# Attention inputs of a hybrid decoder step: three 128-partition transfers per head in place of six 64-partition ones

## The chip, the core and the metric

The kernel runs on one core of one Trainium2 chip. Its engines are TensorE (PE in the profile; PEld is its weight load), VectorE (DVE), ScalarE (ACT), GpSimd (POOL) and SyncE (SP), beside 16 DMA engines that all queues share. Transfers issued by GpSimd appear in the profile as queue q0 (software_dynamic), those issued by SyncE as q1 (hardware_dynamic). The metric is the device time of one execution in microseconds (us); lower is better.

## The reference, cut to what matters

One layer of inference for 2048 new prompt tokens and 8 sample tokens, model width 1024, all float32. The projection of the normalised input gives q, k and v of 16 heads of 64 values each, a gate, and the inputs of a state-space branch. What matters here is the attention of the prompt: each query reads keys at distances 0, d, ..., window for three pairs (window, dilation) and the three results are merged.

```python
PATTERNS = ((128, 1), (512, 4), (2048, 16))
q = _rmsnorm(q.reshape(heads), q_norm_w)
k = _rmsnorm(k.reshape(heads), k_norm_w)
...
s = jnp.einsum('nqhd,nkhd->nhqk', qi, ki).astype(jnp.float32) * scale + bias
s = jnp.where(valid, s, -jnp.inf)
lse = jax.nn.logsumexp(s, axis=-1)
p = jnp.exp(s - lse[..., None]).astype(vi.dtype)
o = jnp.einsum('nhqk,nkhd->nqhd', p, vi)
...
a = o_attn.reshape(lead + (D_ATTN,)).astype(jnp.float32) * jax.nn.silu(g.astype(jnp.float32))
return x + mixed @ w_out
```

## The kernel before

The program is five stages with a barrier between them: `project`, `attend`, `scan_a`, `decode`, `output`. `project` leaves the normalised q and k in DRAM, split into a high and a low part and transposed, as `scr["qk"]` of shape (4, 1024, 2048): entry 0 is q high, 1 is q low, 2 is k high, 3 is k low; head h owns rows 64h to 64h+63, each row 2048 floats (8192 bytes).

`attend` works head by head, h = 0 to 15. A score needs q high and q low against k high and k low. For that q_st holds q high in partitions 0 to 63 and q low in partitions 64 to 127, while k_hi and k_lo each hold the same 64 rows twice, in both halves; a product over 128 partitions then sums both parts of q (lines 1105 and 1106). All three tiles have two buffers, by h % 2.

Order of the work around the change:

- GpSimd issues the loads. `load_qk(h)` (line 1023) waits until the scores of head h-2 are done, since they read the same buffer, and then issues six transfers of 64 partitions (line 1032). Heads 0, 1 and 2 are loaded at the start of the stage, head h+3 within head h, after `apply_gate(h-1)`. Behind it in GpSimd's order stand a load of v (lines 904 and 906: v_in has three copies, one for each dilation, and one load serves two heads), `invert(h-1)` (line 1043) and `normalise(h-1)` (line 1047).
- TensorE, in `scores(h)`, waits at the first unit of a head for `qk_loaded`. Heads 0 and 1 are scored ahead; the scores of head h+2 are interleaved with `mix(h)`, in which the exponentials are turned and multiplied with v.
- The denominator of a head makes a round trip over DRAM, issued by SyncE in order: den out (963), den_in back (967), then GpSimd inverts, reciprocal out (971), reciprocal back to 64 partitions (975), GpSimd normalises, result stored to `mT` (979). Only then does SyncE come to the row maxima of the next head but one (`tops_out`, 937 to 957), whose return, `ntop_loaded`, releases the exponentials of that head and also the next `load_qk`.
- ScalarE starts head h's accumulator with a copy (1289) that waits until head h-2's result is stored, since acc has two buffers.

Two lines elsewhere are read for comparison: line 1526 in `scan_a`, a load that GpSimd issues to all 128 partitions of the tile ya, with a source written as 4 groups of 32 rows:

```python
return bass.AP(tensor=ap.tensor, offset=(512 * (t // 4) + 4 * (t % 4)) * D + i % 2 * HALF, ap=[[D, 4], [16 * D, 32], [1, HALF]])
```

and the loads of the cached keys in `decode`, which go to 128 partitions with a source of 128 rows.

Of the kernel before, what the change touches and what calls it, by code (L numbers as in the profile page):

```python
# [21 lines left out]
F32 = mybir.dt.float32  # L22
# [6 lines left out]
D = 1024  # L29
SEQ = 2048  # L30
# [5 lines left out]
HD = 64  # L36
# [18 lines left out]
def with_axes(ap, axes, offset=0):  # L55

    return bass.AP(tensor=ap.tensor, offset=ap.offset + offset, ap=[list(ap.ap[0])] + [list(a) for a in axes])
# [735 lines left out]
def attend(nc, io, scr):  # L793
# [45 lines left out]
    with ExitStack() as ctx:  # L839
        def sb(name, shape, dt=F32):  # L840
            return ctx.enter_context(nc.sbuf_tensor(name, shape, dt))

        ident = sb("ident_a", [P, P])
        q_st = sb("q_st", [P, 2, SEQ], F32R)
        k_hi = sb("k_hi", [P, 2, SEQ], F32R)
        k_lo = sb("k_lo", [P, 2, SEQ], F32R)
# [21 lines left out]
        qk_loaded = [sem(f"qk_loaded{b}") for b in range(2)]  # L868
# [29 lines left out]
        def load_v(eng, p, j):  # L898

            src = v_src(p, j)  # L900
            dst = v_in[:, p, HD:HD + TILES * (P + 1)].rearrange("i (t c) -> i t c", c=P + 1)[:, :, 0:P]
            if p == 1:
                for b in range(4):
                    eng.dma_start(dst[:, 4 * b:4 * b + 4, :], src[:, b, :, :]).then_inc(v_loaded[p], 16)
            else:
                eng.dma_start(dst, src).then_inc(v_loaded[p], 16)
# [3 lines left out]
        def o_rows(b):  # L910
            return slice(HD * (1 - b), HD * (2 - b))
# [111 lines left out]
        @block.gpsimd  # L1023
        def _(pool):
            def load_qk(h):

                if h >= 2:
                    pool.wait_ge(front_ready, scores_end[h - 2])
                for half in range(2):
                    rows = slice(half * HD, (half + 1) * HD)  # L1030
                    for dst, x in ((q_st, half), (k_hi, 2), (k_lo, 3)):
                        pool.dma_start(dst[rows, h % 2, :].bitcast(F32), scr["qk"][x, h * HD:(h + 1) * HD, :]).then_inc(qk_loaded[h % 2], 16)

            def apply_gate(h, b, pair):

                pool.wait_ge(o_out[0], 4 * h + 8)
                pool.wait_ge(gate_loaded, 32 * (pair + 1))
                pool.tensor_tensor(acc[o_rows(b), b, :], acc[o_rows(b), b, :], gate[o_rows(b), :], ALU.mult).then_inc(gated, 1)
                pool.wait_ge(gated, h + 1)

            def invert(h):
                pool.wait_ge(den_moved, 64 * h + 32)
                pool.tensor_tensor(den_in[:, :], den_in[:, :], minus_one[:, :], ALU.pow).then_inc(recip_done, 1)

            def normalise(h, b):
                pool.wait_ge(den_moved, 64 * h + 64)
                pool.tensor_tensor(acc[o_rows(b), b, :], acc[o_rows(b), b, :], recip[o_rows(b), :], ALU.mult).then_inc(finished, 1)
                pool.wait_ge(finished, h + 1)

            for h in range(2):  # L1050
                load_qk(h)
            pool.memset(v_in[:, :, 0:HD - 1], 0.0).then_inc(ones_set, 1)
            pool.memset(v_in[:, :, VW - HD:VW], 0.0).then_inc(ones_set, 1)
            pool.memset(with_axes(v_in[:, 0, 0:1], [[VW, 3], [P + 1, TILES + 1]], HD - 1), 1.0).then_inc(ones_set, 1)
            pool.memset(minus_one[:, :], -1.0).then_inc(ones_set, 1)
            pool.wait_ge(ones_set, 4)
            for p in (2, 1, 0):
                load_v(pool, p, 0)
            load_qk(2)
            for h in range(H):  # L1060
                if h >= 1:
                    apply_gate(h - 1, (h - 1) % 2, (h - 1) // 2)
                if h >= 2 and h % 2 == 0:
                    pool.wait_ge(mixed, NG * h)
                    load_v(pool, 0, h // 2)
                if h + 3 < H:
                    pool.wait_ge(ntop_loaded, 32 * (h + 2))
                    load_qk(h + 3)
                if h % 2 == 1 and h + 1 < H:
                    pool.wait_ge(mixed, NG * h + 4)  # L1070
                    load_v(pool, 2, (h + 1) // 2)
                if h >= 1:
                    invert(h - 1)
                if h % 2 == 1 and h + 1 < H:
                    pool.wait_ge(mixed, NG * h + 12)
                    load_v(pool, 1, (h + 1) // 2)
                if h >= 1:
                    normalise(h - 1, (h - 1) % 2)
            apply_gate(H - 1, 1, H // 2 - 1)
            invert(H - 1)  # L1080
            normalise(H - 1, 1)

        @block.tensor
        def _(pe):
            def front_bank(n_before, b):
                pe.wait_ge(front_free, n_before + 1)
                return front[b]

            def scores(h, units=range(UNITS)):
                b = h % 2  # L1090
                if 0 in units:
                    pe.wait_ge(qk_loaded[b], 96 * (h // 2 + 1))
                for u in units:
                    at = place["score", h, u]
                    bank = front_bank(at, at % 2)
                    for s in range(2):
                        p, r, blk, _, prev = tiles[2 * u + s]
                        d = DILATIONS[p]
                        lhs = with_axes(q_st[:, b, 0:1], [[d, P]], P * d * blk + r)
                        if p == 2:  # L1100
                            axes, first = [[1, 2], [16, P]], r - r % 2
                        else:
                            axes, first = [[d, 2 * P]], P * d * max(blk - 1, 0) + r
                        out = bank[:, 2 * P * s:2 * P * (s + 1)]
                        pe.matmul(out, lhs, with_axes(k_hi[:, b, 0:1], axes, first), start=True, stop=False)  # L1105
                        last = pe.matmul(out, lhs, with_axes(k_lo[:, b, 0:1], axes, first), start=False, stop=True)  # L1106
                    last.then_inc(front_ready, 1)
# [15 lines left out]
            def mix(h, b, pair, more=True):  # L1123
# [29 lines left out]
                for g in range(NG + 1):  # L1153
                    if g < NG:
                        turn_lot(g)
                    if g == OUT_AT and h + 1 < H:
                        maxima_out(h + 1)
                    if g == IN_AT and h + 1 < H:
                        maxima_in(h + 1)
                    if more:  # L1160
                        scores(h + 2, units_at.get(g, ()))
                    if g >= 1:
                        multiply(g - 1)

            pe.wait_ge(const_in, 16)
            scores(0)
            maxima_out(0)
            scores(1)
            maxima_in(0)
            for h in range(H):  # L1170
# [1291 lines left out]
```

## Time and profile before

| | us |
|---|---|
| median of 3 runs | 3069.5 (3068.41 to 3078.42) |
| the profiled execution, own time | 3077.13 |
| its span | 3075.5 |
| `attend` in it, from the first load issued to the next stage's first instructions | 1367.5 to 2191.5 |
| TensorE busy over the span | 2683.0 (87%) |

The profile is one execution. Its busy times are sums over a stage; its waits name for each idle stretch of an engine what ended it. The DMA share is the mean busy share of the 16 DMA engines, so 0.50 can be eight engines that work all the time. Of a queue the profile gives megabytes and the time its packets took as a share of 16 engines; the two together give the rate of an engine while it is busy.

### The profile page before, as it was taken

How to read it: one execution, taken by the hardware profiler on the slowest of the kernel's cores; microseconds unless marked ns; L12 is line 12 of the kernel's file. 1: busy time of each engine (PE TensorE's matmuls, PEld its weight loads, DVE VectorE, ACT ScalarE, POOL GpSimd, SP SyncE). 2: the span in 40 equal slices, each digit the busy share in tenths (PEclk: the TensorE clock that was granted, in tenths of full speed). 3: DMA queues.
4: the chain of work that ended last, by engine and by line, in shares of the span. 5: the costliest groups of instructions: out<-in, count | busy, mean ns of one | idle time of the engine just before them, and what ended most of it. 6: DMA issues, size and time to landing. Idle time of an engine off the chain costs nothing. (4 is left out here: it accounts for less than half of the span.)

```text
span 3075.5 us, 43713 instructions
## 1 busy us (share of the span) xinstructions
PE 2683.0 (87%) x16598; PEld 2368.4 (77%) x16598; DVE 1236.7 (40%) x3327; ACT 884.2 (29%) x1935; POOL 875.4 (28%) x679
## 2 busy tenths in 40 slices
PE   7799999999999999977999999999269999405799
PEld 7799999999988888846998889988157777302585
DVE  3245554200000045424656566565245555273321
ACT  3212222222111111112545455456044444100100
POOL 1054555221221222210243433434223333141000
PEclk9999999999999999987999999999689999757899
DMA  4224354421231111126556656563455555383632
GB/s 158 85 70 111 105 147 139 131 71 58 73 121 69 68 55 56 55 76 147 126 122 150 147 132 155 126 145 85 109 173 180 184 168 165 124 323 116 218 148 75
DMA packets 197764, 381.87 MB, mean 124 GB/s; under 512 B 62659, under 2 KB 119979, under 8 KB 184476
## 3 DMA queue, kind: packets, MB, share of 16 engines
q1 hardware_dynamic: 158748, 242.40, 25.3%
q0 software_dynamic: 36160, 132.25, 16.9%
q10 hardware_dynamic: 2672, 4.74, 0.5%
q8 instruction: 119, 1.95, 0.3%
q14 instruction: 65, 0.53, 0.1%
HBM read 259.71 MB, written 124.96 MB: 125 GB/s over the span
## 5 line engine op out<-in xcount | busy, mean ns | idle before, releaser
L118 PE MATMUL bank<-w_hi,hT_hi 128*128 128x256 f32 x1792 | 508.0, 283 | 14.2 <-DMA ident<-ident 11.8
L120 PE MATMUL bank<-w_hi,hT_lo 128*128 128x256 f32 x1792 | 504.7, 282 | 0.0
L119 PE MATMUL bank<-w_lo,hT_hi 128*128 128x256 f32 x1792 | 503.2, 281 | 0.0
L1105 PE MATMUL front<-k_hi,q_st 128*128 128x256 f32 x768 | 316.9, 421 | 42.4 <-DMA k_lo<-qk 29.6
L118 PEld LDWEIGHTS bank<-w_hi,hT_hi 128*128 128x128 f32 x1792 | 338.8, 189 | 15.1 <-DMA ident<-ident 12.1
L1148 PE MATMUL obank<-turned_p,v_in 128*128 128x128 f32 (+1 forms) x1632 | 321.5, 331 | 25.9 <-ACT turned_p L1281 24.8
L120 PEld LDWEIGHTS bank<-w_hi,hT_lo 128*128 128x128 f32 x1792 | 339.2, 189 | 0.0
L119 PEld LDWEIGHTS bank<-w_lo,hT_hi 128*128 128x128 f32 x1792 | 338.7, 189 | 0.0
L1148 PEld LDWEIGHTS obank<-turned_p,v_in 128*128 128x128 f32 x1632 | 271.1, 197 | 44.5 <-ACT turned_p L1281 27.5
L1268 ACT ACTIVATE score<-score,ntop_sb 128x256 f32<-128x256 f32 (+1 forms) x768 | 289.9, 455 | 6.7 <-DMA ntop_t<-ntop 6.5
L1106 PE MATMUL front<-k_lo,q_st 128*128 128x256 f32 x768 | 274.5, 365 | 0.0
L118 PE MATMUL bank<-hT_hi,w_hi 128*128 128x512 f32 (+1 forms) x672 | 265.9, 396 | 0.0
L120 PE MATMUL bank<-hT_hi,w_lo 128*128 128x512 f32 (+1 forms) x672 | 265.7, 395 | 0.0
L119 PE MATMUL bank<-hT_lo,w_hi 128*128 128x512 f32 (+1 forms) x672 | 264.1, 393 | 0.0
L403 POOL TENSOR_TENSOR w_hi<-w_raw,zero 128x256 fp32r<-128x256 f32 (+1 forms) x80 | 100.7, 1259 | 562.1 <-PE bank_s L120 303.9
L1195 DVE CUSTOM_DVE_ANT_0 score<-front,bias_sb 128x256 f32<-128x256 f32 (+1 forms) x768 | 249.3, 363 | 14.0 <-issue 13.1
L1105 PEld LDWEIGHTS front<-k_hi,q_st 128*128 128x128 f32 x768 | 209.9, 273 | 51.4 <-issue 30.0
L1106 PEld LDWEIGHTS front<-k_lo,q_st 128*128 128x128 f32 x768 | 214.3, 279 | 0.0
L1132 PE MATMUL back<-ident_a,score 128*128 128x128 f32 x1200 | 186.0, 276 | 0.0
L420 POOL TENSOR_TENSOR rsq<-msq,mhalf 128x4 f32<-128x4 f32 x128 | 129.5, 1012 | 195.9 <-DVE msq L609 195.7
L1281 ACT COPY turned_p<-back 128x512 f32<-128x512 f32 (+1 forms) x160 | 88.4, 553 | 258.0 <-PE back L1132 257.9
L1132 PEld LDWEIGHTS back<-ident_a,score 128*128 128x128 f32 x1200 | 148.1, 143 | 11.9 <-issue 0.2
(282 smaller groups left out, 4824.5 us busy)
## 6 DMA issues: line engine op xcount, KB each, us to landing
qk<-xc_in SPq DMA_DIRECT2D x64, 512.0 KB, 5.1
w_raw<-w_in POOLq DMA_DIRECT2D x26, 1024.0 KB
q_st<-qk POOLq DMA_DIRECT2D x32, 512.0 KB
k_hi<-qk POOLq DMA_DIRECT2D x32, 512.0 KB
k_lo<-qk POOLq DMA_DIRECT2D x32, 512.0 KB
v_in<-v_out POOLq DMA_DIRECT2D x16, 1024.0 KB, 12.9
cum_all<-cum SPq DMA_DIRECT2D x16, 1024.0 KB, 10.4
xcT<-xc SPq DMA_DIRECT2D x12, 1024.0 KB
```

What stands on the lines that cost most here:

```text
L118: pe.matmul(out, lhs_hi(k), rhs_hi(k), start=k == 0, stop=False)
L119: pe.matmul(out, lhs_hi(k), rhs_lo(k), start=False, stop=False)
L120: last = pe.matmul(out, lhs_lo(k), rhs_hi(k), start=False, stop=k == KT - 1)
L403: pool.tensor_tensor(w_hi[:, b, ks, 0:width], w_raw[:, b, ks, 0:width], with_axes(zero[:, :], [[0, n], [0, width]]), ALU.add).then_inc(w_h ...
L420: pool.tensor_tensor(rsq[:, n % 2, :], msq[:, n % 2, :], mhalf[:, :], ALU.pow).then_inc(q_root, 1)
L1105: pe.matmul(out, lhs, with_axes(k_hi[:, b, 0:1], axes, first), start=True, stop=False)
L1106: last = pe.matmul(out, lhs, with_axes(k_lo[:, b, 0:1], axes, first), start=False, stop=True)
L1132: last = pe.transpose(back[g % 2][:, n * P:(n + 1) * P], score[:, b, at:at + P], ident[:, :])
L1148: last = pe.matmul(obank[m["bank"]][:, m["col"]:m["col"] + m["n"]], v_in[:, p, (P + 1) * m["v"][1] + P * b:(P + 1) * m["v"][1] + P * b + P ...
L1195: last = dve.tensor_tensor_reduce(out=score[:, b, at:at + w], in0=front[place_at % 2][:, 2 * P * s + skip:2 * P * s + skip + w], in1=bias[ ...
L1268: act.activation(score[:, b, at:at + w], score[:, b, at:at + w], ACTF.Exp, bias=ntop[:, b, n:n + 1]).then_inc(exp_done, 1)
L1281: act.copy(turned_p[:, g % 4, 0:n], back[1][:, 0:n]).then_inc(odd_out, 1)
```

## The change

`load_qk` issues three transfers, each to all 128 partitions. The source is written as two groups of 64 rows: for q_st the groups lie 1024 rows apart (q high and q low), for k_hi and k_lo the step between the groups is 0, so the same 64 rows are read twice. The bytes are the same, 3.15 MB a head. `scores` waits for 48 in place of 96 on the semaphore.

```diff
                 if h >= 2:
                     pool.wait_ge(front_ready, scores_end[h - 2])
-                for half in range(2):
-                    rows = slice(half * HD, (half + 1) * HD)
-                    for dst, x in ((q_st, half), (k_hi, 2), (k_lo, 3)):
-                        pool.dma_start(dst[rows, h % 2, :].bitcast(F32), scr["qk"][x, h * HD:(h + 1) * HD, :]).then_inc(qk_loaded[h % 2], 16)
+                for dst, x, apart in ((q_st, 0, D * SEQ), (k_hi, 2, 0), (k_lo, 3, 0)):
+                    first = scr["qk"][x, h * HD:(h + 1) * HD, :]
+                    src = bass.AP(tensor=first.tensor, offset=first.offset, ap=[[apart, 2], [SEQ, HD], [1, SEQ]])
+                    pool.dma_start(dst[:, h % 2, :].bitcast(F32), src).then_inc(qk_loaded[h % 2], 16)
...
                 if 0 in units:
-                    pe.wait_ge(qk_loaded[b], 96 * (h // 2 + 1))
+                    pe.wait_ge(qk_loaded[b], 48 * (h // 2 + 1))
```

The order on TensorE, VectorE, ScalarE and SyncE is unchanged. On GpSimd, inside one head of `attend` (here the loads of a head, then of v, then invert; names are tile<-source and the destination's shape), before:

```order
L1038 TENSOR_TENSOR acc<-acc,gate 64x2048
L1032 DMA q_st<-qk 64x2048
L1032 DMA k_hi<-qk 64x2048
L1032 DMA k_lo<-qk 64x2048
L1032 DMA q_st<-qk 64x2048
L1032 DMA k_hi<-qk 64x2048
L1032 DMA k_lo<-qk 64x2048
L906 DMA v_in<-v_out 128x16x128
L1043 TENSOR_TENSOR den_in<-den_in,minus_one 128x16
```

and after, at the same place on GpSimd:

```order
L1038 TENSOR_TENSOR acc<-acc,gate 64x2048
L1032 DMA q_st<-qk 128x1x2048
L1032 DMA k_hi<-qk 128x1x2048
L1032 DMA k_lo<-qk 128x1x2048
L906 DMA v_in<-v_out 128x16x128
L1043 TENSOR_TENSOR den_in<-den_in,minus_one 128x16
```

Six issues became three and nothing else moved; over the 16 heads GpSimd issues 48 transfers in place of 96. In `scan_a`, further on in GpSimd's list and the same in both kernels, stands the load of ya, which has the same form as the new transfers:

```order
L1521 DMA ma_raw<-mT 128x1024
L1526 DMA ya<-x_all 128x1x512
L1521 DMA ma_raw<-mT 128x1024
L1526 DMA ya<-x_all 128x1x512
```

Nothing moved here; the rows are shown for the shape of ya's transfer.

## Rows read from the trace of the kernel before

**Rows 1.** The page: each engine's busy time and its share of the span.
```profile
PE 2683.0 (87%) x16598; PEld 2368.4 (77%) x16598; DVE 1236.7 (40%) x3327; ACT 884.2 (29%) x1935; POOL 875.4 (28%) x679
```

**Rows 2.** Windows: stretch, length, busy by engine, granted clock, DMA share, GB/s.
```profile
1366.00:1396.00 30.00, 3.78 (x16) 3.62 (x16) 1.57 (x15) 0.00 (x0) 12.10 (x22) 0.50 0.94 206
...
1500.00:1600.00 100.00, 97.35 (x601) 92.72 (x600) 59.65 (x304) 53.71 (x135) 33.42 (x24) 1.00 0.59 136
```

**Rows 3.** TensorE's waits from 1366 to 1500: us in total, times, longest.
```profile
PE front L1105 <- DMA k_lo<-qk: 29.6, 1, 29.6
PE front L1105 <- DVE top L1195: 10.3, 10, 8.3
```

**Rows 4.** Timeline: GpSimd's first load issued, and TensorE's first score.
```profile
1367.49 0.56 POOL L1032 DMA_DIRECT2D q_st<-qk  x1 [70.57 <-POOLq L2353]
...
1392.22 0.56 PE L1105 MATMUL front<-k_hi,q_st 128*128 128x256 f32 x1 [29.64 <-DMA k_lo<-qk]
```

**Rows 5.** Timeline: head 0's maxima sent by SyncE, and back at VectorE.
```profile
1416.10 0.94 SPq L937 DMA_DIRECT2D tops<-top  x2
...
1433.43 0.21 DVE L1214 TENSOR_REDUCE top<-tops_sb 128x16 f32<-128x48 f32 x1 [8.90 <-DMA tops_sb<-tops]
```

**Rows 6.** DMA queues, 1612 to 1620, a load of q and k: packets, MB, share.
```profile
q0 software_dynamic: 260, 1.70, 102.0%
```

**Rows 7.** DMA queues, 2750 to 2790, loads to 128 partitions in `decode`.
```profile
q1 hardware_dynamic: 720, 6.29, 41.2%
```

**Rows 8.** The last two loads of ya: GpSimd's issue, a window, q0 from 2616 to 2624.
```profile
2613.92 1.42 POOL L1526 DMA_DIRECT2D ya<-x_all  x2 [0.30 <-POOL xend L1540]
...
2618.00:2621.00 3.00, 3.00 (x15) 2.49 (x14) 0.00 (x0) 0.00 (x0) 1.74 (x1) 1.00 0.49 135
...
q0 software_dynamic: 544, 0.53, 29.1%
```

**Rows 9.** Timelines of SyncE and GpSimd over two heads.
```profile
1614.26 0.32 SPq L971 DMA_DIRECT2D den<-den_in  x1
1625.85 0.46 SPq L975 DMA_DIRECT2D recip<-den  x1
...
1662.14 0.32 SPq L971 DMA_DIRECT2D den<-den_in  x1
1673.80 0.46 SPq L975 DMA_DIRECT2D recip<-den  x1
...
1606.51 0.60 POOL L1032 DMA_DIRECT2D q_st<-qk  x1 [4.21 <-issue]
...
1635.35 4.55 POOL L1047 TENSOR_TENSOR acc<-acc,recip 64x2048 f32<-64x2048 f32 x1 [14.99 <-DMA recip<-den]
...
1656.06 0.55 POOL L1032 DMA_DIRECT2D q_st<-qk  x1 [10.04 <-DMA ntop_t<-ntop]
...
1678.72 4.56 POOL L1047 TENSOR_TENSOR acc<-acc,recip 64x2048 f32<-64x2048 f32 x1 [16.60 <-DMA recip<-den]
...
1702.20 0.60 POOL L1032 DMA_DIRECT2D q_st<-qk  x1 [4.18 <-issue]
```

**Rows 10.** Timelines, the same steps for head 13, with no load in flight.
```profile
2127.66 0.33 SPq L971 DMA_DIRECT2D den<-den_in  x1
2129.07 0.46 SPq L975 DMA_DIRECT2D recip<-den  x1
...
2133.80 4.53 POOL L1047 TENSOR_TENSOR acc<-acc,recip 64x2048 f32<-64x2048 f32 x1 [6.16 <-DMA recip<-den]
```

**Rows 11.** Waits: TensorE from 1500 to 2190, ScalarE and SyncE from 1500 to 2100.
```profile
PE obank L1148 <- ACT turned_p L1281: 24.8, 9, 4.4
...
ACT acc L1289 <- DMA mT<-acc: 68.9, 12, 9.4
...
SPq L975 <- DMA den<-den_in: 135.3, 13, 11.6
SPq L950 <- DVE ntop_sb L1216: 66.8, 13, 10.4
```

## The prediction, as it was put on record

> **What bounds the kernel now.** I read the page first, then the stage that the change touches, and there the waits. TensorE is busy for 87% of the span [rows 1]; over most of `attend` it is at 97% [rows 2], so a transfer is worth time only where TensorE ends up waiting for it. Three such places exist. (a) At the start of the stage TensorE does nothing until head 0's q and k are there: 29.6 us [rows 3], of which 24.7 us lie between the first load issued at 1367.49 and the first score at 1392.22 [rows 4]; the DMA engines are 94% busy in that stretch (the first of [rows 2]). (b) The first row maxima go out at 1416.10 and are back at 1433.43 [rows 5], 17.3 us for a few kilobytes, and TensorE waits 8.3 of them [rows 3]. (c) After that TensorE never waits for q or k. It waits for a ScalarE copy, 24.8 us in nine places [rows 11], up to 4.4 each, and these stand behind ScalarE's wait for a stored head, 68.9 us in twelve places, up to 9.4. That stored head is the end of the round trip of the denominator, which SyncE issues step by step, so the round trip must be followed.
>
> Rows 9 show it for two heads. With a load of q and k in flight the 8 KB reciprocal takes 11.6 us from its issue to the next issue, in both heads (1614.26 to 1625.85, 1662.14 to 1673.80). With nothing in flight the same step takes 1.4 us [rows 10]. The way back to 64 partitions takes 9.5 us where loads of v are still moving (1625.85 to 1635.35), 4.9 us where the load is over (1673.80 to 1678.72), and 4.7 us in a quiet stretch [rows 10]. Because SyncE works in order, and its list leads on to the row maxima that release the next load, these latencies are in the loop that sets the pace of a pair of heads, 1606.51 to 1702.20 = 95.7 us [rows 9]. The loop has little slack: SyncE waits 66.8/13 = 5.1 us a head for VectorE [rows 11], and not all of that is free.
>
> **What the change does to a load.** The bytes stay. What decides is how many DMA engines carry a transfer and how fast each goes.
>
> Before: from 1612 to 1620 the queue moved 1.70 MB at 102% of 16 engines [rows 6], 1.70/(1.02 x 16 x 8 us) = 13.0 GB/s an engine. To 128 partitions engines do better: 6.29 MB at 41.2% over 40 us [rows 7] is 6.29/(0.412 x 16 x 40) = 23.9 GB/s. So 64 partitions cost about half the rate of an engine, and the change takes that handicap away. A head's 3.15 MB take 3.15/(16 x 0.0130) = 15.1 us now.
>
> After: the nearest row is the load of ya, also issued by GpSimd, also to 128x1xN, with a source in 4 groups. Two of them are in flight from 2618 to 2621, and the DMA share is 0.49 at 135 GB/s [rows 8], eight engines of sixteen: four for each, and two different sets of four. Groups and engines have the same number. The new source has 2 groups, so I take two engines for a transfer, and a different pair for each of the three: six engines for a head. The Trainium skill (DMA: Bandwidth & Descriptors, "Why a DMA increments its semaphore by 16 and not by 1") says that a DMA gets the largest number up to 16 that divides the slowest dimension on both sides, which gives 2 here and 4 for ya. By that rule the row and the forecast agree.
>
> Each of the six engines then carries 3.15/6 = 0.524 MB. At 23.9 GB/s that is 21.9 us. But ya's engines ran slower: 0.53 MB for 29.1% of 16 engines over 8 us [rows 8] is 14.2 GB/s, and at that rate it is 36.9 us; at the 13.0 of rows 6 it would be 40. Why narrow transfers that run side by side are slow the rows do not tell; three that start together and walk through the partitions in the same order may get in each other's way. Bounds 22 and 37 us; I take 29, halfway, because ya's short transfers carry their start-up in that rate. The load of a head gets longer by 14 us although the handicap is gone.
>
> **The sum.** (a) Start: now 24.7 us. After: about 1.5 us until data flow, 29 us for head 0 (head 1 goes to the next six engines at the same time), and a share of SyncE's bias and gate loads, 1.77 MB or 0.11 MB an engine, 4.6 us at 23.9 and 8.5 at 13.0, of which I take 5. Together 35.5: **+11 us**. Bounds 1.5 + 22 + 4.6 = 28, +3.4; 1.5 + 37 + 8.5 = 47, +22.
>
> (b) First maxima: now 17.3 us under a load on all 16 engines. Six busy engines with a quicker pace each should delay less. Between 0 and the 8.3 of the wait I take **-3 us**.
>
> (c) Each of the other loads is issued one head (48 us) before its scores, so even 37 us are hidden. Their cover is that distance; it would be gone at 48. What remains is what a load does to the reciprocal's steps. Such a step needs all the engines, so the slowest counts, and 11.6 - 1.4 = 10.2 us of delay are 16 packets of 8192 bytes at 0.63 us (8192 bytes at 13.0 GB/s). At 29 us for 64 packets a packet takes 0.45, so the delay is 16 x 0.45 = 7.2: the step out takes 8.6, **-3.0** in each head. But the load now lasts into the step back. Where that took 4.9 it takes 4.7 + 7.2 = 11.9, **+7.0**; where it took 9.5, **+2.4**. The maxima after it meet the tail of v's loads, which wait behind q and k on the six engines: I take **+1** a pair. A pair of heads: -6.0 + 7.0 + 2.4 + 1 = +4.4. GpSimd saves three issues of 0.5 us; they stand ahead of a step that waits for other things in one head of two, and I count nothing. From the fourth load to the last there are 12, six pairs, and v's loads extend it a little: 6.5 x 4.4 = **+29 us**.
>
> At 22 us a load: a packet 0.34, delay 5.5; -4.7 twice, +5.3 and +0.7: -3.4 a pair, -22 in all. At 37 us: 0.58, delay 9.3; -0.9 twice, +9.1, +4.5, and up to +4 for the maxima: +16, or +104. So (c) is the large term and its sign turns at a load of about 24 us.
>
> Sum: +11 - 3 + 29 = **+37 us**. On the profiled execution's 3077.1 that is 3114; that execution stands 7.6 us (0.25%) over the median of 3069.5, so on the median **3107 us**.
>
> **Rivals.**
> 1. *The narrow transfers run at full rate* (22 us). For it: rows 7. Against: ya's rate in rows 8. Start +3.4, maxima -3, pairs -22: -22 us, 3048. TensorE can gain no more in a pair than it waits there, some 4 us, so it does not go much lower. This is the case that ends faster; it decides below a load of 24 us.
> 2. *The three transfers crowd each other fully* (37 us). For it: 14.2 GB/s in rows 8. Start +22, pairs +104: about +120, 3190.
> 3. *The transfer is spread over all sixteen engines*, as its 128 destination partitions suggest. Then 3.15 MB take 3.15/(16 x 0.0239) = 8.2 us, the start gets some 10 us shorter (4.9 MB with SyncE's loads in 12.9 + 1.5 against 24.7), the first maxima 5, and the reciprocal is out of the load's way, so that TensorE's 24.8 us go: -40, 3030. Against it: 0.49 for two transfers in rows 8. The Trainium skill (DMA: Bandwidth & Descriptors, "Rules for kernel authors") advises one 128-partition transfer in place of two to disjoint halves. By that rule the time would be this rival's; the same list warns that a slowest dimension under 16 confines a transfer to as many engines.
> 4. *It does not matter*: shorter delay and longer load cancel in (c), with (a) small; a load of 24 to 26 us, 3060 to 3079.
>
> That all three share one pair (66 us a load, no longer hidden behind 48) is ruled out by the two sets of four in rows 8 as far as ya goes; it would cost over 200 us.
>
> **How the numbers follow.** Forecast (load 26 to 34 us) 0.50, rival 2 with all above 34 us 0.20, rival 1 0.14, rival 3 0.06, rival 4 0.10. What a measurement of this kernel can tell from no change is about 0.3%, 9 us. Faster by more: 0.20; within: 0.12 (rival 4 and the edge of the forecast); slower: 0.68. The likeliest case gives 3107, its own range 3080 to 3150. For 8 in 10 the range reaches into rival 1 and to most of rival 2: 3045 to 3180.
>
> **What the profile after would show.** Two engines each: while a load is in flight alone the DMA share is near 6/16 = 0.38 (0.75 when heads 0 and 1 load together), not 1.0; a share of 1.0 at twice the rate would be rival 3. The first score would come 35 us after the first load is issued. SyncE's wait before line 975 would fall from 11.6 to about 9, and GpSimd's before line 1047 rise in the heads where it is short now. The distance between load issues of two heads apart would grow from 95.7 to 100; if it shrinks, (c) has the wrong sign. If TensorE waits for k_lo in later heads too, the loads are longer than a head. I would be wrong most of all if the rate of narrow transfers is not between the two rows, or if the delay of a small transfer is not in proportion to the time of a packet.

## The result, and the profile of the changed kernel

The changed kernel takes 3219.4 us (median of 4 runs, 3213.4 to 3228.1), the kernel before 3071.9 in the same comparison: 1.048 times as long, 95% interval 1.0449 to 1.0511. The direction was forecast, the size was not: +148 us where +37 was expected, and outside the range. The profiled execution has a span of 3226.5 us, 151 more than that of before.

The page first, TensorE's row (it answers to [rows 1]) and the row of GpSimd's queue: packets, MB, share of 16 engines.

```profile
PE 2691.5 (83%) x16598; PEld 2374.5 (74%) x16598; DVE 1231.8 (38%) x3327; ACT 884.6 (27%) x1935; POOL 865.0 (27%) x631
...
q0 software_dynamic: 78400, 132.42, 15.9%
```

TensorE does the same work in 8.5 us more; the rest of the 151 is idle time. (The packets more than doubled, while the megabytes stayed; more on that at the end.) The waits over the stage, from 1366 to 2350, of TensorE, ScalarE and SyncE (us in total, times, longest), beside [rows 3, 11]:

```profile
PE front L1105 <- DMA k_lo<-qk: 179.0, 14, 70.5
PE front L1105 <- DVE top L1195: 21.1, 9, 19.4
PE obank L1148 <- ACT turned_p L1281: 10.2, 9, 2.2
...
ACT acc L1289 <- DMA mT<-acc: 38.9, 7, 6.9
...
SPq L975 <- DMA den<-den_in: 122.0, 16, 13.7
```

The first row carries the result. Before, TensorE waited for k_lo once, 29.6 us; now fourteen times, 179.0 us. One of these is the start (70.5); the other thirteen, one in each later head from the fourth on (head 3, as heads count from 0), sum to 108.5, or 8.3 each. Against [rows 3] the first maxima cost 11.1 us more (19.4 for 8.3), and against [rows 11] the waits for ScalarE's copy are 14.6 us less. So 40.9 + 108.5 + 11.1 - 14.6 + 8.5 = 154 against the 151 us of the span: the loss is located.

The 8.5 us of busy time fit the waits. After head 6's wait of 8.61 us the granted clock is at the lower of its two levels (0.50, 1.2 GHz) for over 4 us, where the kernel before, which does not wait there, has 1.00 (2.4 GHz). The first 4 us with head 6's scores, after and then before (18 matmuls for 21):

```profile
1717.00:1721.00 4.00, 3.91 (x18) 3.74 (x19) 1.53 (x11) 0.92 (x3) 3.48 (x2) 0.50 0.70 178
...
1631.00:1635.00 4.00, 3.80 (x21) 3.52 (x20) 2.61 (x13) 1.39 (x3) 0.00 (x0) 1.00 0.38 69
```

The start, beside [rows 4]: GpSimd's first issue, and TensorE's first score.

```profile
1369.22 0.85 POOL L1032 DMA_DIRECT2D q_st<-qk  x1 [70.56 <-POOLq L2353]
...
1434.79 0.56 PE L1105 MATMUL front<-k_hi,q_st 128*128 128x256 f32 x1 [70.46 <-DMA k_lo<-qk]
```

From issue to score 65.6 us, where it was 24.7. One later load, head 5's:

```profile
1632.83 0.83 POOL L1032 DMA_DIRECT2D q_st<-qk  x1 [18.64 <-DMA ntop_t<-ntop]
...
1662.61 0.59 PE L1105 MATMUL front<-k_hi,q_st 128*128 128x256 f32 x1 [3.85 <-DMA k_lo<-qk]
```

Issue to score is 29.8 us here, and TensorE was late by 3.85. For the next four loads it is 34.4, 31.8, 36.5 and 30.5, always ended by k_lo. Over all thirteen it is 29.8 to 32.7 us in the odd heads and 34.4 to 40.5 in the even ones, where five of v's loads are issued while the load runs; the mean is 34.3. Less TensorE's wait, 25.1 to 26.5 us are left: that is when TensorE would have come to use the data. In the kernel before, head 6 was loaded at 1606.51 and head 7 at 1656.06 [rows 9], and this is TensorE's first score with each:

```profile
1631.04 0.55 PE L1105 MATMUL front<-k_hi,q_st 128*128 128x256 f32 x1
...
1681.97 0.55 PE L1105 MATMUL front<-k_hi,q_st 128*128 128x256 f32 x1
```

No wait is marked, yet the distance from issue to use is 24.5 and 25.9 us, not 48 (23.9 to 26.2 over the thirteen heads). That distance is all the time that a load has before it holds up TensorE; it is called its cover below.

Last, windows (stretch, length, busy by engine, granted clock, DMA share, GB/s): the start, and five microseconds of the later load in which nothing else moves.

```profile
1390.00:1410.00 20.00, 0.00 (x0) 0.00 (x0) 0.00 (x0) 0.00 (x0) 0.00 (x0) 0.50 1.03 124
...
1642.00:1647.00 5.00, 5.00 (x35) 4.78 (x34) 4.18 (x18) 2.60 (x9) 0.00 (x0) 1.00 0.38 158
```

0.38 is six engines of sixteen, as forecast, and 158/6 is 26 GB/s for each. At the start all sixteen are busy, with less moved.

### The profile page after: what moved, and what is told of

Its sections match the earlier page's. It is cut to its first block and busy times, and to the rows that moved or that the text cites. A ratio compares the mean times of both kernels' runs of the same rounds, so it can differ in the third digit from the quotient of the medians.

```text
span 3226.5 us, 43665 instructions
## 1 busy us (share of the span) xinstructions
PE 2691.5 (83%) x16598; PEld 2374.5 (74%) x16598; DVE 1231.8 (38%) x3327; ACT 884.6 (27%) x1935; POOL 865.0 (27%) x631
## 3 DMA queue, kind: packets, MB, share of 16 engines
q0 software_dynamic: 78400, 132.42, 15.9%
## 5 line engine op out<-in xcount | busy, mean ns | idle before, releaser
L1105 PE MATMUL front<-k_hi,q_st 128*128 128x256 f32 x768 | 318.0, 422 | 200.3 <-DMA k_lo<-qk 179.0
L118 PEld LDWEIGHTS bank<-w_hi,hT_hi 128*128 128x128 f32 x1792 | 338.7, 189 | 15.3 <-DMA ident<-ident 11.9
L1148 PEld LDWEIGHTS obank<-turned_p,v_in 128*128 128x128 f32 x1632 | 271.5, 198 | 29.7 <-ACT turned_p L1281 12.9
L1195 DVE CUSTOM_DVE_ANT_0 score<-front,bias_sb 128x256 f32<-128x256 f32 (+1 forms) x768 | 249.3, 363 | 13.9 <-issue 13.0
L1188 DVE MEMSET tick<- 128x1 f32 x384 | 22.7, 59 | 378.4 <-PE front L1106 374.8
```

Source lines behind the costliest of these rows:

```text
L118: pe.matmul(out, lhs_hi(k), rhs_hi(k), start=k == 0, stop=False)
L1148: last = pe.matmul(obank[m["bank"]][:, m["col"]:m["col"] + m["n"]], v_in[:, p, (P + 1) * m["v"][1] + P * b:(P + 1) * m["v"][1] + P * b + P ...
L1195: last = dve.tensor_tensor_reduce(out=score[:, b, at:at + w], in0=front[place_at % 2][:, 2 * P * s + skip:2 * P * s + skip + w], in1=bias[ ...
```

## The experiments

Theory after the result: the source's slowest dimension of 2 gives each transfer two engines (such a transfer is called narrow below); the load of a head then takes 30 to 40 us, longer than the 24 to 26 us from its issue to its use, and at the start two such loads and v's slow each other.

**swap**: the three transfers with the 64 rows as the slowest dimension and the two copies inside. The two copies of a row then lie in adjacent partitions, for q and k alike, so the products are unchanged.

```diff
-                    src = bass.AP(tensor=first.tensor, offset=first.offset, ap=[[apart, 2], [SEQ, HD], [1, SEQ]])
+                    src = bass.AP(tensor=first.tensor, offset=first.offset, ap=[[SEQ, HD], [apart, 2], [1, SEQ]])
```

> The changed kernel with one edit: the source's two outer dimensions change places, so it is 64 groups of 2 rows in place of 2 groups of 64, and partition 2i+half holds row i of that half, in q_st, k_hi and k_lo alike. Bytes, issues, destination and waits are the same. Theory (the number of groups sets the number of DMA engines): the load is carried by 16 engines, DMA share near 1.0 while it is in flight, 3.15 MB in 8 to 10 us; first score about 15 us after the first issue; no later wait for k_lo; time 3020 to 3050. Rival (three transfers to 128 partitions are slow as such): the loads stay at 30 to 36 us and the time near 3219.

Measured 3036.3 us, ratio to before 0.9874 (0.9845 to 0.9904), as the theory had it. Its window in a later load, and its waits from 1366 to 2650:

```profile
1640.00:1645.00 5.00, 5.00 (x28) 4.87 (x28) 3.56 (x15) 2.60 (x10) 1.14 (x1) 1.00 1.02 425
...
PE front L1105 <- DMA k_lo<-qk: 23.8, 1, 23.8
PE front L1105 <- DVE top L1195: 7.6, 23, 3.1
PE obank L1148 <- ACT turned_p L1281: 3.2, 4, 1.5
```

Same tiles, same bytes, same three transfers; only the order of the source's dimensions differs. All sixteen engines work, 425 GB/s instead of 158 (and instead of the 210 that [rows 6] give for 64 partitions). The start, the first maxima and ScalarE's copies all cost TensorE less than before: 5.8 + 5.2 + 21.6 us. So the whole loss of the change comes from the order of the source's dimensions, with which go the number of engines and the partitions that each of them writes; and this kernel is 1.3% faster than the one before.

**early**: the changed kernel, with each later load issued at the start of its head, without waiting for the row maxima. This gives the cover of about a head that the prediction had assumed.

```diff
             for h in range(H):
+                if h + 3 < H:
+                    load_qk(h + 3)
...
-                if h + 3 < H:
-                    pool.wait_ge(ntop_loaded, 32 * (h + 2))
-                    load_qk(h + 3)
```

> The changed kernel with load_qk(h+3) issued at the head's start, ahead of apply_gate and without its wait for ntop_loaded (the wait for the scores of head h+1 stays). Theory (a load of 33 us is covered by only 26 us): with some 45 us of cover the 13 later waits for k_lo, 108 us, go, the start stays slow: about 3120, up to 3150 if the earlier load delays the row maxima. Rival (the waits come from the DMA engines being full, so that a load takes as long as the head however early it is issued): waits and time stay near 3219.

Measured 3286.9 us, 1.0691 (1.0664 to 1.0719). The expectation failed, and the rows say how (1366 to 2650):

```profile
PE obank L1147 <- DVE turned_p L1226: 158.6, 15, 25.6
PE front L1104 <- DMA k_lo<-qk: 68.7, 1, 68.7
...
DVE top L1213 <- DMA tops_sb<-tops: 215.4, 14, 28.5
...
SPq L945 <- DMA tops<-top_t: 187.8, 16, 30.0
SPq L975 <- DMA den<-den_in: 17.1, 16, 1.1
```

The thirteen later waits for k_lo are gone, with 52 to 73 us from issue to use: more distance is what they lacked. But the load now lies over the row maxima's way over DRAM, where each small step waits behind it, and TensorE waits for the exponentials instead, 158.6 us. The denominator's step, clear of the load, is down to 1.1 us.

**before_early** does the same to the kernel before.

> The kernel before, with each later load issued at the start of its head, without waiting for the row maxima. The step from den to its reciprocal should come down from 11.6 us to 1.4, as in the run early. If the collision with the row maxima goes by the load's length (15 us here against 30 to 36 in early, which lost 50 us to the changed kernel), the maxima's way back grows by 8 to 12 us a head, of which SyncE's slack of some 5 us a head takes a part: 3080 to 3150. Rival (only loads that outlast the cover collide): 3050 to 3073.

Measured 3077.4, ratio 1.0007 (0.9991 to 1.0024): no difference, and between the two cases of the expectation (3080 to 3150, 3050 to 3073). SyncE's wait for den falls from 138.5 us to 17.8 (16 times each, from 1366 on), its wait at line 945 rises from 54.3 to 113.5, VectorE's wait for the maxima from 12.1 to 66.2, and TensorE's waits only change their name: 22.4 us for VectorE's copy in place of 24.8 for ScalarE's. A load delays whichever round trip it lies on. Moving a load of 15 us is a draw, moving one of 30 or more a loss.

**swap_early** puts the early issue on swap.

> The source of the three transfers written with the 64 rows outside and the two copies inside (as in the run swap, 3036), and besides each later load issued at the start of its head, without waiting for the row maxima. If the collision seen in the run early (small transfers delayed behind a load) scales with the load's length, a load of some 10 to 15 us at full width now lies beside the row maxima's way back: that step grows from about 7 to 12 to 15 us in each head and the kernel takes 3036 + 0 to 40, that is 3035 to 3075. Rival (the early issue takes the load out of the denominator's way, which is what ScalarE and TensorE still wait for): 3015 to 3030.

Measured 3032.7, ratio 0.9853 (0.982 to 0.9886), which overlaps swap's interval; it lies between the two cases expected. With a load of some 8 us neither place hurts: the den step falls from 77.4 to 18.7 us in 16, the maxima's rises from 27.5 to 80.8, and TensorE waits for neither.

**start_only** and **rest_only** divide the change by heads: the three narrow transfers for heads 0 and 1 alone, or for all heads but these, and six transfers for the others.

```diff
+                if h < 2:
+                    for dst, x, apart in ((q_st, 0, D * SEQ), (k_hi, 2, 0), (k_lo, 3, 0)):
...
+                else:
+                    for half in range(2):
...
```

> Three transfers for heads 0 and 1, the old six for heads 2 to 15. Theory (the start costs 41 us and the first row maxima 11, by the traces): 3072 + 50 = 3122, first score 65 us after the first issue. Rival (the start overlaps with what follows and is given back): under 3100.

Measured 3135.8, 1.0194 (1.0155 to 1.0233): 62 us, where 50 were expected. The profile shows the start at 62.5 us from issue to score (1368.58 to 1431.09), the first wait 67.4 (+37.8), 12 us more of TensorE's busy time, and 12 us more of a wait in `scan_a` that no part of the change touches (acc_a, 42.1 for 30.1; it lies between 23 and 42 in these profiles). The first maxima cost 8.6, as before.

> The old six transfers for heads 0 and 1, three for heads 2 to 15. Theory (13 waits for k_lo of 8.3 us each, 108 us, less some 15 us of ScalarE's stalls that go): 3072 + 95 = 3167. Rival (the later waits follow from the late start): close to 3072.

Measured 3206.5, 1.043 (1.0404 to 1.0456): 133 us, where 95 were expected. Two rows from 1366 to 2650:

```profile
PE front L1111 <- DMA k_lo<-qk: 133.7, 14, 29.6
PE front L1111 <- DVE top L1201: 21.1, 10, 19.2
```

The start is as before (29.6), the thirteen others are 104.1 us, and the first maxima wait 19.2. So that last loss belongs to head 2's narrow load, in flight while they travel, and not to those of heads 0 and 1. The two parts sum to 195 us and the whole is 148, so shares are read from the waits and not from these differences. On the profiled executions the parts are 63 and 120 us, 32 more than the 151 of the whole. Of this excess 20 us are waits in `scan_a` (12 and 7 more than before, and 1 less in the changed kernel) and 20 are TensorE's busy time (12.2 and 16.5 more, against 8.5); 7.5 go the other way, as both parts together wait less for k_lo. Why the wait in `scan_a` differs was not found.

**in_turn** and **offset** ask what makes the start slow. in_turn issues head 1's load when head 0's is complete; offset issues it behind v's first loads, 8.7 us after head 0's.

```diff
-            for h in range(2):
-                load_qk(h)
+            load_qk(0)
+            pool.wait_ge(qk_loaded[0], 48)
+            load_qk(1)
```

> The changed kernel, with the load of head 1 issued only when head 0's is complete; nothing else differs. Theory (narrow transfers that are in flight together slow each other, so that 12 engines for two heads take 60 us where a head alone takes 30 to 36): the first score comes 32 to 38 us after the first load is issued instead of 65.6, TensorE's first wait is about 40 us instead of 70.5, a second wait of 5 to 20 us for k_lo follows at head 1, and the kernel takes 3219 - 30 + 12 = about 3200 (3190 to 3210). Rival (a pair of engines is that slow from the stage's other traffic, v's load and SyncE's, or from the first touch of the rows): the first score still comes over 55 us after the issue, head 1 is later still, and the kernel takes 3240 or more.

in_turn took 3209.0 us, 1.0437 (1.0401 to 1.0472), and its first score came 34.3 us after the first issue (1368.01 to 1402.30). Without head 1's load and v's beside it, a head takes at the start what it takes later. Part of the gain goes to a second wait of 13.9 us at head 1.

> The changed kernel, with the load of head 1 issued behind the first loads of v instead of ahead of them, some 8 us later; nothing waits. Theory (transfers that walk through the same partitions at the same moment slow each other, whatever their number): 8 us or more apart, heads 0 and 1 share twelve engines at nearly full pace, the first score comes 30 to 40 us after the first load is issued instead of 65.6, and while both heads load the rate is over 180 GB/s where it was 124 to 137. The kernel takes 3219 - 20 = about 3200 (3185 to 3210), somewhat below in_turn. Rival (it is the number of narrow transfers in flight that counts): the first score comes 50 us or more after the issue, the rate stays under 150 GB/s, and the kernel takes 3210 to 3225.

offset took 3208.9, 1.0414 (1.039 to 1.0437), which the theory's range still holds, but its first score and rate did not come: the first score 54.8 us after the issue (1368.47 to 1423.24), 120 GB/s from 1400 to 1410. An offset of 8.7 us does not free the two heads from each other; the theory of two loads that meet at the same partitions falls in this form. It also clears v, whose loads in_turn had held back together with head 1's: by the sizes of the packets, v's (4096 bytes) move 3 of these 120 GB/s, and q's and k's (8192 bytes) 116. But twelve narrow engines aren't always slow: in in_turn, when the end of head 1's load meets the start of head 2's, the window reads

```profile
1430.00:1435.00 5.00, 0.00 (x0) 0.00 (x0) 0.00 (x0) 0.00 (x0) 0.00 (x0) 0.50 0.74 263
```

twelve engines (0.74) at 22 GB/s each.

**one_narrow**: the kernel before, only k_lo as one narrow transfer behind the four others.

```diff
-                    for dst, x in ((q_st, half), (k_hi, 2), (k_lo, 3)):
+                    for dst, x in ((q_st, half), (k_hi, 2)):
                         pool.dma_start(dst[rows, h % 2, :].bitcast(F32), scr["qk"][x, h * HD:(h + 1) * HD, :]).then_inc(qk_loaded[h % 2], 16)
+                first = scr["qk"][3, h * HD:(h + 1) * HD, :]
+                src = bass.AP(tensor=first.tensor, offset=first.offset, ap=[[0, 2], [SEQ, HD], [1, SEQ]])
+                pool.dma_start(k_lo[:, h % 2, :].bitcast(F32), src).then_inc(qk_loaded[h % 2], 16)
```

> The kernel before, with only k_lo's two transfers of 64 partitions replaced by the narrow one of 128 (q_st and k_hi stay as four transfers on all engines). Theory (three narrow transfers side by side slow each other): alone, a pair of engines carries its 0.52 MB each in 22 to 25 us plus its sixteenth part of the other four transfers, 0.13 MB each or 5 to 10 us, partly overlapped: the load takes 26 to 30 us, which meets the cover of 26 to 28, so the later waits for k_lo stay under 3 us each, and the kernel takes 3075 to 3110. Rival (a pair of engines is slow by itself, 32 us or more for a transfer whatever runs beside it): the load takes 35 us or more, TensorE waits some 8 to 10 us for k_lo in each of 13 heads, and the kernel takes 3180 to 3220.

Measured 3253.9, 1.0574 (1.0529 to 1.0618), worse than three narrow ones, and outside both expectations. Two windows of one load, issued from 1613.92 on:

```profile
1616.00:1626.00 10.00, 10.00 (x58) 9.72 (x57) 7.60 (x31) 5.04 (x16) 3.79 (x3) 1.00 0.96 196
...
1636.00:1641.00 5.00, 3.23 (x24) 2.83 (x22) 3.31 (x12) 1.97 (x5) 3.13 (x1) 1.00 0.12 52
```

First the four wide transfers go on sixteen engines; then two engines (0.12) carry k_lo alone at 26 GB/s each. The pair is not slow: 1.05 MB at 52 GB/s are 20 us. But they come after the 10 us of the others and not beside them, and TensorE waits 152 us in thirteen heads. The expectation had them partly overlapped; here the narrow transfer waits its turn on its engines.

**six_g2**: the kernel before, its six transfers to 64 partitions with each source as 2 groups of 32 rows.

```diff
-                        pool.dma_start(dst[rows, h % 2, :].bitcast(F32), scr["qk"][x, h * HD:(h + 1) * HD, :]).then_inc(qk_loaded[h % 2], 16)
+                        first = scr["qk"][x, h * HD:(h + 1) * HD, :]
+                        src = bass.AP(tensor=first.tensor, offset=first.offset, ap=[[SEQ, 2], [2 * SEQ, HD // 2], [1, SEQ]])
+                        pool.dma_start(dst[rows, h % 2, :].bitcast(F32), src).then_inc(qk_loaded[h % 2], 16)
```

> The kernel before with its six transfers to 64 partitions, but each source written as 2 groups of 32 rows (even rows, then odd rows, the same for q and k, so the products are the same). Theory (the slowest dimension of the source sets the number of engines and each transfer gets another pair): the six transfers of a head take twelve engines, 0.26 MB each; at 13.0 GB/s 20 us, at 26 GB/s 10 us, so the load takes 12 to 22 us, DMA share about 0.75 while it lasts, later waits for k_lo are absent or small, and the kernel takes 3040 to 3100. Rival A (pairs are shared between the halves, six engines a head): 30 us or more, waits for k_lo of 4 to 14 us in each head, 3180 to 3230. Rival B (the 128 partitions mattered, not the groups: 64 partitions keep all 16 engines): DMA share 1.0 during a load, 3065 to 3080.

Measured 3655.4 us, 1.1872 (1.1841 to 1.1904), worse than every expectation. A stretch of the start (with a second load in flight), and one of head 5's load, issued at 1746.50, which is alone:

```profile
1410.00:1430.00 20.00, 0.02 (x1) 0.05 (x1) 0.00 (x0) 0.00 (x0) 0.00 (x0) 0.50 1.24 65
...
1770.00:1780.00 10.00, 0.00 (x0) 0.00 (x0) 0.84 (x2) 0.00 (x0) 0.00 (x0) 0.66 0.79 68
```

Twelve engines (0.79) move 65 to 68 GB/s together, less than half of what six moved in the changed kernel, and a later load takes 57 to 64 us from issue to score. (Of the 1.24 at the start 0.46 are packets of 4 bytes; the 8192-byte packets of q and k are 0.76.) The groups alone, without any transfer to 128 partitions, are enough to ruin the load. Why the pace collapses was still open, and three runs separate source from destination: theory S puts it down to the rows that are read, theory D to the partitions that are written.

**six_near** keeps six_g2's destinations and lets the source step by one row (row 63 is left out).

```diff
-ap=[[SEQ, 2], [2 * SEQ, HD // 2], [1, SEQ]]
+ap=[[(HD // 2 - 1) * SEQ, 2], [SEQ, HD // 2], [1, SEQ]]
```

> The run six_g2 with the same destinations, but the two groups of a source are rows 0 to 31 and rows 31 to 62 (step 1 row inside a group in place of 2); row 63 is left out, so the products are not the reference's. Theory S (the slow pace comes from the source: rows read at the same time in steps of 16 KB): the rate during a load rises from 75 to over 140 GB/s, the load takes under 25 us, later waits for k_lo are small, and the kernel takes 3050 to 3150. Theory D (it comes from the partitions written at the same time, here i, 32+i, 64+i and 96+i): the rate stays at 70 to 85 GB/s and the kernel takes 3600 to 3700. If the groups are merged into one, the DMA share is 1.0 at 210 GB/s and the run says nothing.

Measured 3667.6 (1.1922, interval 1.1862 to 1.1982), and 60 GB/s in the same stretch of the start: theory D, though its rate is below the 70 to 85 GB/s expected.

**stride2** keeps the changed kernel's destinations and lets the source step by two rows (`[2 * SEQ, HD]`), so it reads rows of other heads too.

> The changed kernel with every second row of twice the range as its source (step 16 KB in place of 8 KB), so the values are not the reference's; destinations, bytes and engines are the same. Theory S: the rate of a later load falls from some 140 to 158 GB/s to 75 to 90, the load takes 40 us or more in place of 30 to 36, the waits for k_lo grow by 8 us or more a head, and the kernel takes 3330 to 3450. Theory D: nothing changes, 3200 to 3235.

Measured 3236.6 (1.0521, interval 1.0463 to 1.0579), first score after 66.3 us, waits for k_lo 195.7 us for 179.0: little of the 110 us and more that theory S asked for. 15.5 of the 16.7 us come from head 14 alone (29.7 for 14.2), which waits longer in far_rows too (21.1); the other twelve heads wait 94.8 us for 94.4.

**far_rows** takes head 1's rows from head 9.

> The changed kernel with head 1's rows taken from head 9 (4 MB further on), so its values are not the reference's; destinations, bytes, order and engines are the same. Theory S in its narrow form (heads 0 and 1 read rows half a megabyte apart in step, and that is what slows them): the first score comes 35 to 50 us after the first load is issued instead of 65.6. Theory D, or a limit on twelve narrow transfers whatever they read: 60 us or more, and the kernel takes 3205 to 3230.

Measured 3221.6 (1.0472, interval 1.0387 to 1.0557), first score after 64.3 us: theory D again. What is read, and how far apart, hardly matters. Nor is it the number of engines or of transfers alone: a lone load of six_g2 and the window of in_turn both have twelve engines and six transfers, at 68 and 263 GB/s. What is left is where, and how far apart in time, narrow transfers write. Which rule holds there was not found.

The three last runs have two executions each; six_near, stride2 and far_rows compute other values than the reference, by the rows that they read.

## Why the prediction was wrong, point by point

1. *How many engines*: right. 0.38 in a lone load, two engines a transfer, six a head. Rival 3 is dead as written, but its mechanism was real and needs the other order of the source: swap reads 1.02 and 425 GB/s, and takes 3036 where that rival said 3030.
2. *How long a load takes*: 29 us was forecast between 22 and 37, with 1.5 before it until data flow; issue to score is 29.8 to 40.5, on average 34.3, so it was some 4 us short. The lone pace is 26 GB/s an engine, nearer to the upper row of the two (23.9). What adds 10 us and more to the 3.15/0.158 = 20 us is taken to be the issue and what shares the engines, v's and SyncE's transfers; no run separates them.
3. *"Each of the other loads is issued one head (48 us) before its scores, so even 37 us are hidden"*: **this is the step that failed.** 48 us is the distance between two loads. The distance from a load's issue to the first score that reads it was not read from the trace; it is 24.5 and 25.9 us, since GpSimd's list issues the load behind the gate and its wait for the row maxima (18.64 us of idle time in the row above, ended by ntop_t; in the even heads the row names no releaser), and not when the buffer comes free. Issued at the start of its head, as in early, it had distance enough. A load of 30 to 40 us outlasts that by 4 to 14 us, thirteen times: 108.5 us. The prediction's own sign ("if TensorE waits for k_lo in later heads too, the loads are longer than a head") had the right row and the wrong threshold. With the cover of 25 us, the forecast's own 29 us give 13 x 4 = 52 us more, a total of +89 and 3159, still 60 below the measurement; the measured mean of 34.3 less the 25.9 that TensorE left it gives 13 x 8.4 = 109. So about half of the term is the cover, and half is the load that was longer than forecast (point 2).
4. *The start*: +11, with 22 as the upper bound; measured +40.9. The mis-sized term is head 0's load, because heads 0 and 1 do not go "at the same time" at full pace: loaded together, head 0 is there after 65.6 us, alone after 34.3 (in_turn), and with v's loads ahead of head 1's still after 54.8 (offset). Their twelve engines and v's four move 124 GB/s. A row gave a warning that was used for a single head only: eight engines of ya made 135 GB/s [rows 8], 17 each and not 24.
5. *First maxima*: forecast -3, measured +11.1. The sign was wrong: the length of the load that lies over the small transfers outweighed the engines that it leaves free. rest_only pins it on head 2's load. With swap's short load the same wait is 3.1.
6. *The denominator's steps*: right in the steps, wrong in what they cost. In the twelve heads with a load in flight the step out (from line 971 to 975) fell from 11.5 to 10.1 us on average (forecast 8.6), and the step back (from 975 to GpSimd's line 1047) rose from 7.0 to 10.5 (forecast 11.9 in every head). That is +4.2 us for a pair of heads, where these steps were forecast at +3.4. But the +29 us for TensorE did not appear; its waits for ScalarE fell by 14.6. The likely reason is that a TensorE that is held up for k_lo gives the round trip time, so that a cost beside a larger wait of the same loop is not added to it.

The direction came out, but in part by luck: the terms that make the loss, the later waits and most of the start, are not those from which the forecast took it, and its largest term, +29 in the denominator's steps, cost TensorE nothing. The range failed because all its cases took point 3 for granted.

## What to carry to other kernels

Before lengthening a transfer, read its cover from the trace: the time from its issue to the first instruction that uses its data, not the period of the loop. Write the source of a DMA so that its slowest dimension is large (here 64 rows outside, 2 copies inside); the other order of the same bytes cost 6% of this kernel, the right one gained 1.3%. Several small round trips in a loop are delayed by the length of whatever bulk load lies on them, so shorten the load before moving it.

## What the runs showed of the hardware

- The slowest dimension of the source sets the number of engines. That dimension was 2 in the changed kernel and 64 in swap, with 128 destination partitions in both: 0.38 (three transfers) and 1.02 of the DMA engines. The Trainium skill (DMA: Bandwidth & Descriptors, "Why a DMA increments its semaphore by 16 and not by 1") states this rule: the largest number up to 16 that divides the slowest dimension on both sides. These runs agree.
- In transfers to 128 partitions an engine moves 26 GB/s, whether two, six or sixteen engines are at work (52, 158 and 425 GB/s); sixteen engines writing to 64 partitions move 13 GB/s each [rows 6].
- Narrow transfers can slow each other far below that. Twelve engines in six_g2 move less than half of what six do in the changed kernel, also in a lone load (68 GB/s), and it is not the source (six_near, 60). A load of v on other engines is slow beside them: at the start all sixteen are busy at 124 GB/s.
- A large load delays small transfers of the other queue. SyncE's step from line 971 to 975 takes 1.4 us alone [rows 10], 11.5 under a load of 15 us and 6.7 to 14.0 under the changed kernel's loads.
- GpSimd's queue has 36160 packets of 132.25 MB before, 35392 in swap and 78400 of 132.42 MB in the changed kernel: 42240 more packets in 0.17 MB, 4 bytes each. Narrow transfers bring them along; whether they cost time no run shows.
- A narrow transfer behind wide ones in GpSimd's queue starts on its engines when they are done, not beside them (one_narrow: 196 GB/s for 10 us, and 52 at the end).
- GpSimd needs 0.8 us to issue a narrow transfer, and 0.5 to 0.6 for each of before's; three took 2.4 us, six 3.1.
